# Row sums of two Strassen-type FFNs made pair by pair, a first up unit in 8 products, and squares added on VectorE

## The reference, cut to what matters

```python
def _swiglu(h, w1, w3, w2):
    return (jax.nn.silu(h @ w1) * (h @ w3)) @ w2          # FFN2: D_FF = 2816

u = rmsnorm(x, norm_mlp_g[i]) @ w_up[i]                   # FFN3: D_FF_2 = 4096
x = x + jnp.square(jax.nn.relu(u)) @ w_down[i]
```

```python
xf * lax.rsqrt(jnp.mean(xf * xf, axis=-1, keepdims=True) + EPS)
```

## Time and profile before

| What | Value |
|---|---|
| Median of 3 runs | 3257.37 us (3256.01 to 3264.33) |
| The profiled execution, its own time | 3262.65 us |
| Its span in the trace | 3261.0 us |
| TensorE matmuls busy | 3027.8 us (93%) |
| DVE, ACT, POOL busy | 1029.3, 445.8, 416.3 us |
| FFN2, first to last unit start | 1550.84 to 1967.56 us |
| FFN3, first to last unit start | 2734.95 to 3145.63 us |

### The profile page before, as it was taken

One profiled execution on the slowest core, in us unless ns is written; L12 is line 12 of the kernel. 1 busy time (PEld: TensorE's weight loads), 2 busy tenths in 40 slices (PEclk: granted clock), 3 DMA queues, 4 the chain that ended last, 5 costly groups with the idle time before them and its releaser, 6 DMA issues.

```text
span 3261.0 us, 26581 instructions
## 1 busy us (share of the span) xinstructions
PE 3027.8 (93%) x10626; PEld 1897.7 (58%) x10626; DVE 1029.3 (32%) x1857; ACT 445.8 (14%) x968; POOL 416.3 (13%) x362
## 2 busy tenths in 40 slices
PE   3999999997999999998999998997889998999998
PEld 1555555553556457443888884754444445888873
DVE  6222225004005534002332335107550003343432
ACT  2000000002004334002100001004330000000001
POOL 0000000000002000001344440000000002444420
PEclk8999999998999999999999999998999999999999
DMA  6222224111110100221222221210002221222211
GB/s 249 88 98 99 101 99 135 66 55 39 52 45 8 30 20 11 78 78 51 78 79 89 78 78 57 72 67 14 26 28 83 77 78 65 78 78 78 78 58 58
DMA packets 42521, 228.10 MB, mean 70 GB/s; under 512 B 4144, under 2 KB 6448, under 8 KB 26928
## 3 DMA queue, kind: packets, MB, share of 16 engines
q1 hardware_dynamic: 32768, 181.17, 16.6%
q0 software_dynamic: 8928, 39.85, 3.4%
q10 hardware_dynamic: 720, 5.61, 0.4%
HBM read 224.51 MB, written 2.10 MB: 69 GB/s over the span
## 4 chain that ended last, share of the span: by engine, by line
PE 88%; DVE 8%; ACT 1%; issue 1%; DMA 1%; ACTq 0%; DVEq 0%
PE banks L365 57%; PE banks L430 21%; PE banks L537 1%; PE banks L692 1%; PE banks L612 1%; PE banks L685 1%; DMA consts_sb<-consts 1%; PE banks L374 1%; DVE rstd L1259 1%; PE banks L835 1%; DVE scratch_b L1276 1%; PE banks L602 1%; DVE p_embed L1309 1%; PE banks L417 1%; DVE big L1355 1%
## 5 line engine op out<-in xcount | busy, mean ns | idle before, releaser
L365 PE MATMUL banks<-normed,weight_ring 128*128 128x512 f32 (+2 forms) x3296 | 1199.8, 523 | 49.3 <-ACT normed L916 29.9
L365 PEld LDWEIGHTS banks<-normed,weight_ring 128*128 128x128 f32 (+1 forms) x3296 | 630.6, 192 | 601.5 <-issue 551.7
L365 PE MATMUL banks<-big,weight_ring 128*128 128x512 f32 (+4 forms) x1720 | 626.5, 519 | 8.5 <-DVE big L1448 5.6
L365 PEld LDWEIGHTS banks<-big,weight_ring 128*128 128x128 f32 (+2 forms) x1720 | 321.0, 187 | 300.7 <-issue 273.6
L430 PE MATMUL banks<-big 128*128 128x256 f32 x1776 | 414.4, 389 | 39.1 <-DVE rpb_rows L1370 32.3
L430 PEld LDWEIGHTS banks<-big 128*128 128x128 f32 x1776 | 345.9, 195 | 92.0 <-DVE rpb_rows L1370 25.1
L1825 POOL TENSOR_TENSOR big<-weight_ring 128x512 f32<-128x512 f32 (+1 forms) x66 | 82.7, 1253 | 1216.1 <-PE banks L430 542.4
L430 PE MATMUL banks<-big,weight_ring 128*128 128x256 f32 x736 | 170.9, 381 | 0.0
L430 PEld LDWEIGHTS banks<-big,weight_ring 128*128 128x128 f32 x736 | 140.9, 191 | 19.5
L1309 DVE CUSTOM_DVE_ANT_0 p_embed<-big,rpb_rows 128x1024 f32<-128x1024 f32 x116 | 141.9, 1223 | 24.6 <-DMA big<-w_ada 16.5
L1445 DVE TENSOR_TENSOR scratch_a<-scratch_a,banks 128x512 f32<-128x512 f32 x16 | 11.0, 688 | 356.9 <-ACT scratch_a L1001 356.9
(11 more groups left out here) (261 smaller groups left out, 2435.8 us busy)
## 6 DMA issues: line engine op xcount, KB each, us to landing
weight_ring<-weights SPq DMA_DIRECT2D x136, 1024.0 KB, 4.9
big<-w_ada POOLq DMA_DIRECT2D x42, 512.0 KB, 4.1
weight_ring<-weights SPq DMA_DIRECT2D x20, 768.0 KB, 4.2
weight_ring<-weights SPq DMA_DIRECT2D x16, 704.0 KB, 4.1
big<-w_ada POOLq DMA_DIRECT2D x4, 2048.0 KB, 26.0
rpb_rows<-w_ada POOLq DMA_DIRECT2D x14, 512.0 KB, 4.7
weight_ring<-weights SPq DMA_DIRECT2D x8, 640.0 KB, 3.9
residual<-xT ACTq DMA_DIRECT2D x2, 1536.0 KB, 20.1
```

The lines of the kernel that those rows point to most:

```text
L365: ins = nc.tensor.matmul(o, w, r, start=start, stop=stop)
```

## The change

1. **Pairing.** The two halves of the inner tiles are no longer the first and the last `kp` tiles but the even and the odd ones. A pair of neighbouring tiles can then give its four sums (128x256 each) as soon as both tiles exist. POOL reads the weights with a stride of two tiles; the loads are unchanged.
2. **Pair sums.** DVE makes the four chained operations of a pair (`pair_sums`) right behind the up unit that completes it: after every second up unit in FFN2 (f odd), after every up unit in FFN3. Sums of `HR[0]` and `HR[1]` have a buffer each (one of the four sums is written in place over rows that are no longer needed, another partly in free ends of scratch tensors). The `row_sums` calls between the phases go away.
3. **First unit.** The first up unit of each FFN is made without sums: 16 matmuls of 512 columns, k outermost, two PSUM banks, each k waiting only for its tile of H. The row sums of H (`all_sums`, six operations) are made during it. ACT and DVE finish it with full-width operations (`first_up2`, `first_up3`).
4. **Squares.** In `down1` and `out1` DVE copies the first squared chunk and adds the next six in `TMP`; TensorE makes one ones-matmul per column part from that total and one from the last chunk. `out2` keeps its sums on TensorE.
5. Some semaphores are shared between norms to make room (three `stages` of "norm_late", with bases).

The diff, cut to its core:

```diff
@@ tensor
-                    if sums and not (peel and j == 0):
+                    if sums and sums[0] is not g and not (peel and j == 0):
...
-            def fast(v, rows, t, rows_sem=None, rows_at=0, t_at=None):
+            def fast(v, rows, buffer, totals=None, freed=None):
...
+                def raw(m, j):
+                    return lambda p: slot(n, (m * 2 * kp + 2 * p + j) * P, P)
...
+                def rows_raw(j, l):
+                    return lambda p: rows[:, 2 * p + j, l * HALF:(l + 1) * HALF]
...
+                if freed is not None:
+                    pe.wait_ge(hid, freed)
+                product(za, raw(0, 0), rows_raw(0, 0), True, True)
                 pe.wait_ge(sums, v + 1)
-                if t_at is not None:
-                    pe.wait_ge(hts, t_at + 2)
-                product(zb, w[1], total(1), True)
-                product(zc, w[0], total(0), True)
-                if t_at is not None:
-                    pe.wait_ge(hts, t_at + 3)
+                if totals is not None:
+                    pe.wait_ge(hts, totals)
+                product(zb, total(1), rows_total(1), True)
+                product(zc, total(0), rows_total(0), True)
                 pe.wait_ge(took, 5 * v + 1)
-                product(zb, w[2], total(2), False)
+                product(zb, total(2), rows_total(2), False)
...
+            def first_up(n, s, g):
+                begin(n)
+                for k in range(KC):
+                    pe.wait_ge(g["ready"], g["base"] + k + 1)
+                    for w in range(2):
+                        last = mm(bank[:, 3 * s + w, :], slot(n, (w * KC + k) * P, P), H[:, k, 0:S], k == 0,
+                                  k == KC - 1, k == 0 and w == 0)
+                last.then_inc(first_done, 1)
...
+                if sg is g:
+                    pe.wait_ge(sg["sq_used"], sg["base"] + KC - 1)
+                    for (a, b, _), q in zip(parts, banks):
+                        nc.tensor.matmul(bank[:, q, 0:b - a], ones, TMP[:, 0, a:b], start=True, stop=False)
+                    pe.wait_ge(sg["sq"], sg["base"] + KC)
+                    for (a, b, _), q in zip(parts, banks):
+                        last = nc.tensor.matmul(bank[:, q, 0:b - a], ones, SQ[:, 1, a:b], start=False, stop=True)
...
-            fast_up(range(34, 38), nmlp, 16)
-            fast_up(range(38, 42))
-            fast_down(42, 0, HT, 26, 20)
...
+            first_up(UP3[0], (V_UP3[1] + 1) % 2, nmlp)
+            fast_up([V_UP3[j] for j in range(1, 8)], FF + 1, TOTALS_3[0])
+            fast_down(V_DOWN3[0], 0, FF + 4, TOTALS_3[1])
...
@@ scalar
+            def first_up2(s):
+                act.wait_ge(first_done, 1)
+                A(bias_t[:, 5 * s * HALF:(5 * s + 2) * HALF], bank[:, 3 * s, :], ACT.Silu).then_inc(first_act, 1)
+            def first_up3(s):
+                act.wait_ge(first_done, 2)
+                for w in range(2):
+                    A(HR[0][:, w, :], bank[:, 3 * s + w, :], ACT.Relu).then_inc(first_act, 1)
...
@@ vector
+                def each(i, a, b):
+                    for p, n in groups(i):
+                        V.tensor_tensor(row_sum(buffer, rows, i, p, n), a(p, n), b(p, n),
+                                        ALU.subtract).then_inc(hts, 1)
+                        row_sums_done[0] += 1
+                    return row_sums_done[0]
...
+                at = each(2, lambda p, n: raw(1, 1, p, n), lambda p, n: raw(0, 1, p, n))
+                if buffer < 2:
+                    dve.wait_ge(hts, at)
+                at = each(0, lambda p, n: raw(0, 1, p, n), lambda p, n: raw(0, 0, p, n))
+                dve.wait_ge(hts, at)
+                at = each(1, lambda p, n: raw(1, 1, p, n), total(0))
+                dve.wait_ge(hts, at)
+                each(3, lambda p, n: raw(1, 0, p, n), total(1))
+
+            def pair_sums(i, p):
+                dve.wait_ge(dve_c, chain[0])
+                row_sums_of(i % 2, HR[i % 2], lambda i: [(p, 1)])
+
+            def all_sums():
+                row_sums_of(2, H, lambda i: [(0, 4)] if i > 1 else [(0, 2), (2, 2)])
...
@@ up2_unit
+                if f % 2 == 1:
+                    dve.wait_ge(hid, f + 1)
+                    pair_sums(f // PHASE, f % PHASE // 2)
@@ up3_unit
                 V.scalar_tensor_tensor(rows, rows, 0.0, rows, ALU.max, ALU.mult).then_inc(hid, 1)
+                dve.wait_ge(hid, FF + j + 1)
+                pair_sums(j // 4, j % 4)
...
+            def squares_added(g, width):
+                at = g["base"]
+                dve.wait_ge(g["sq"], at + 1)
+                V.tensor_copy(TMP[:, 0, 0:width], SQ[:, 0, 0:width]).then_inc(g["sq_used"], 1)
+                for o in range(1, KC - 1):
+                    dve.wait_ge(g["sq"], at + o + 1)
+                    dve.wait_ge(g["sq_used"], at + o)
+                    V.tensor_tensor(TMP[:, 0, 0:width], TMP[:, 0, 0:width], SQ[:, o % 2, 0:width],
+                                    ALU.add).then_inc(g["sq_used"], 1)
```

More of the change, by code:

```diff
@@ L80, with _fast, _ups, _downs @@
 DOWN3 = [SEQ["down3a"], SEQ["down3b"], SEQ["down3c"], SEQ["down3d"]]
[L84 to L92, removed]
-def unit_of(v):
[L96 to L103, removed]
+FAST = []
+def _fast(n, kp, copied):
+    FAST.append((n, kp, copied))
+    return len(FAST) - 1
+def _ups(units, a, b):
+    return {f: _fast(units[f], 4, True) for f in range(a, b)}
+def _downs(units, i, kp, copied):
+    return [_fast(units[i] + m, kp, copied) for m in range(4)]
+V_UP2 = _ups(UP2, 1, 16)
+V_DOWN2 = [_downs(DOWN2, 0, 4, True)]
+V_UP2.update(_ups(UP2, 16, FF))
+V_DOWN2 += [_downs(DOWN2, 1, 4, False), _downs(DOWN2, 2, 3, False)]
+V_FFN3 = len(FAST)
+V_UP3 = _ups(UP3, 1, 8)
+V_DOWN3 = [_downs(DOWN3, 0, 4, False)]
+V_UP3.update(_ups(UP3, 8, 12))
+V_DOWN3.append(_downs(DOWN3, 1, 4, False))
+V_UP3.update(_ups(UP3, 12, 16))
+V_DOWN3 += [_downs(DOWN3, 2, 4, False), _downs(DOWN3, 3, 4, False)]
+V_END = len(FAST)
+TOTALS_2 = [6 + 4 * n for n in (0, 4, 8, 11)]
+TOTALS_3 = [TOTALS_2[-1] + 6 + 4 * n for n in (0, 4, 8, 12, 16)]
+def unit_of(v):
+    return FAST[v][0:2]
 def copied_upto(v):
-    return sum(1 for u in range(v + 1) if not any(at <= u < at + 4 for at in V_DOWN2[1:] + V_DOWN3))
+    return sum(1 for u in range(v + 1) if FAST[u][2])
 def _places(columns):
@@ L464, in fast @@
                 pe.wait_ge(took, 5 * v + 3)
-                product(zc, w[3], raw(1, 1), False)
-            def fast_up(vs, normed=None, t_at=None):
-                for v in vs:
[L469 to L477, removed]
+                product(zc, total(3), rows_raw(1, 1), False)
@@ new lines, in first_up, with fast_up @@
+            def first_up(n, s, g):
[6 more added lines that the diff above has]
+                last.then_inc(first_done, 1)
+            def fast_up(vs, hidden=None, totals=None):
+                for i, v in enumerate(vs):
+                    fast(v, H, 2, totals if i == 0 else None, hidden if i == 1 else None)
@@ L479, in squares_total, with fast_down @@
+            def fast_down(vs, i, hidden, totals):
+                pe.wait_ge(hid, hidden)
+                for v in vs:
+                    fast(v, HR[i % 2], i % 2, totals)
             def squares_total(g):
@@ L706, in _ @@
             norm_sums(nb, LAT)
[L708 to L713, removed]
+            first_up(UP2[0], (V_UP2[1] + 1) % 2, nb)
+            fast_up([V_UP2[f] for f in range(1, 16)], 1, TOTALS_2[0])
+            fast_down(V_DOWN2[0], 0, 8, TOTALS_2[1])
+            fast_up([V_UP2[f] for f in range(16, FF)])
+            fast_down(V_DOWN2[1], 1, 16, TOTALS_2[2])
+            fast_down(V_DOWN2[2], 2, 22, TOTALS_2[3])
             squares_total(sq2)
@@ L964, in up2_units @@
                     u2, g1 = tmps(v % 2)[1], tmps(v % 2)[4]
+                    if v == V_UP2[1] + 1:
+                        act.wait_ge(hid, 1)
                     fast_snap(v)
@@ L1500, in _ @@
             link(gate_coef(GATE3, 8, 0.5, 5))
+            squares_added(down1, T)
             dve.wait_ge(down1["free"], KC)
@@ L1594, in _ @@
             merge(mrg1, MR1)
+            squares_added(out1, S)
             dve.wait_ge(out1["free"], 2 * KC)
```

223 lines of the change are left out of this document (110 added, 113 removed).

## The result

The changed kernel takes **3270.28 us** (median of 7 runs, 3269.56 to 3273.73) against 3257.68 for the kernel before (7 runs, 3256.01 to 3264.33): ratio 1.0036, interval 1.0024 to 1.0047, so 12.6 us slower, just past the 9.8 us that a measurement can tell. The profiled spans are 3268.3 us and 3261.0. They differ by 7.3 only, since the profiled execution of before stood 5.0 above the median; sums made from the two traces go against the 7.3.

The account below looks back on a forecast made before the run. TensorE was taken as the bound; 67.2 us removed, 66.6 us of stalls and 8.6 us of clock falls added gave +8.0 us on the 3257.37 median: 3265 us, range 3218 to 3287, most of the chance within 3252 to 3273.

Parts of the forecast that it names:

- The junctions' 47.4 us: Seven FFN units where TensorE waited for row sums: their extra time goes, 47.4 us less.
- the squares' 12.9: Unhidden ones-matmuls in down1 and out1 fall to one on the DVE total: 12.9 us less.
- B1: Rival: pair operations cost a flat 0.755 us, gaps of about 1 us, no clock falls; 3219 us, chance 0.12.
- B2: Rival: pair operations are hidden, at 0.425 us each; 3192 us, chance 0.08.
- D: Rival: openings or squares bring nothing, or a down unit still waits for its totals; 3285 us, chance 0.05.
- POOL's L1828 and L1830 lines longer by about 0.2 us: Sign of being right: these two POOL weight-sum lines lengthen by about 0.2 us.
- Openings: First units of both FFNs: 16.4 us each against 19.74 and 19.89, 6.9 us gained for both.
- Stalls: Fourth product late behind pair sums: 2.9 us 15 times in FFN3, 2.1 us 11 times in FFN2; 66.6 us added.
- the clock: FFN3 stalls let TensorE's clock fall in 6 of 15, at 1.43 us each: 8.6 us added.
- FFN2's part: Clock cost of FFN2's gaps of 1.7 us before the fourth product: put at nothing.
- case A: Forecast case: DVE and POOL take turns, some clock falls; 3257 us without falls, 3271 with ten; chance 0.55.
- C: Rival: the clock falls in nearly every FFN3 stall, 1.43 to 2.64 us each; 3287 us, chance 0.20.

Follow-up runs that it names:

- experiment 6: The kernel before with only the squares of down1 and out1 added on DVE: 3250.10 us, ratio 0.9969.
- Experiments 1 and 2: Changed kernel with POOL starting weight sums three products later: 3191.84 us; changed kernel with pair sums moved behind the next unit's emptying of zb: 3195.52 us.
- experiment 3: Changed kernel with five unread matmuls before the wait of the fourth product in 15 FFN3 units: 3251.84 us, ratio 0.9974.
- experiment 7: The kernel before with POOL starting a unit's weight sums after product 3 of the previous unit: 3221.49 us, ratio 0.9886.

## Why the prediction was right, and where it was off

**Right in the mechanism.** The junctions' 47.4 us went as worked out, and so did the squares' 12.9 (experiment 6 alone: 12.6). The four operations took turns with POOL: 1.37 three times and 0.42, as predicted, starting at U + 2.69 for U + 2.66. The rivals B1 and B2 are excluded by those durations and by the stalls, D by the openings and by experiment 6. Experiments 1 and 2 show the cause: the durations hang on POOL, the time on L1453's place behind them. One point failed: "POOL's L1828 and L1830 lines longer by about 0.2 us". L1924 took 1.44 us in that unit and L1926 1.32, where POOL's operations take 1.27 undisturbed: 0.17 and 0.05 longer, so 0.2 only for the two together.

**Sizes by step.** Openings: 8.0 us gained for 6.9. Against the 13.74 us at full speed, FFN3's (16.33) lost 2.6 and FFN2's (15.33) 1.6, after 5.14 and 5.80 us of idleness; the 2.64 for a slow start, taken from the PLE opening, was right in FFN3 and too much in FFN2. Stalls: 2.65 and 1.87 us for 2.9 and 2.1, so 60.4 for 66.6. Part of that is L1453, which starts 0.08 before the drawn end of the last pair operation (2767.28 against 2762.72 + 4.64 = 2767.36), where I had it 0.04 after; it ends at U + 7.67 for the 7.82 worked out.

**The mis-sized term is the clock.** "Two in five of 15 is 6, at 1.43 each 8.6 us" became 11 at 1.68, 18.5 us, as the trace shows and experiment 3 gives back. The chance of a fall was taken from five single gaps in stages of different work, and two falls in five say little of a rate. The 1.43 was one row's. FFN2's part, "I put at nothing", came out right: none of 11. But one of its reasons was misread, "of the eight like them (1.85 to 1.87) most left the clock up". Six of those gaps stand before L537 in the trace of before, and within 1.6 us of TensorE's return the granted clock was down after five of them, left up only by the one at 2284.06. The windows view from one of the five and from that one:

```profile
2236.82:2244.00 7.18, 6.72 (x46) 4.09 (x46) 6.13 (x23) 3.65 (x15) 0.00 (x0) 0.76 0.01 2
```

```profile
2284.00:2291.00 7.00, 5.57 (x46) 3.21 (x46) 6.48 (x27) 4.09 (x18) 0.00 (x0) 1.00 0.01 2
```

The stage of these gaps has more and shorter bursts of matmuls than FFN2. Read rightly, its rows spoke for falls in FFN2, and that none came there was luck.

By these steps the sum is -47.4 - 8.0 - 12.9 + 39.8 + 20.6 + 18.5 = +10.6 us for the +8.0 predicted; with -3.1 in stages whose code did not change it is 7.5, beside the 7.3 of the spans. That the total came so near is in part luck: stalls that were 6.2 us cheaper and openings that were 1.1 us better than predicted hid most of the 9.9 us that the clock cost more. So it is case A as to the time ("with ten 3271"), with the falls in number on C's side of its point ("from eight falls on"), at a price near the lower end of C's. Compared by the medians of 7 runs the kernel is 12.6 us slower, past the 0.3%, and the forecast of "same" was on the wrong side of that line by 2.8 us; the clock's 9.9 us were enough to carry it there. Against the medians beside the experiments (7.6 to 8.6 us) it was on the right side.

**What stays open.** Why 4 of 15 equal stalls of 2.38 us left the clock up was not tried. No run moved a gap on purpose, but two did so in passing. The gap of 2.82 us in the earlier trace rows (1464.95) left the clock up, 14.00 us for its 32 records. In experiment 7, whose code is the same up to there, it came 2.8 us sooner and the clock fell (first row below). The gap of 3.69 us in FFN2 was followed by a fall in the kernel before (second row, granted clock 0.66 in the 5 us from there), and by none in experiment 6 (third row, 1.00):

```profile
1462.12 15.45 PE L365 MATMUL banks<-big,weight_ring 128*128 128x512 f32 x32 [2.82 <-DVE big L1448]
```

```profile
1895.44 2.38 PE L430 MATMUL banks<-big 128*128 128x256 f32 x8 [3.69 <-DVE rpb_rows L1370]
```

```profile
1885.09 1.97 PE L430 MATMUL banks<-big 128*128 128x256 f32 x8 [3.69 <-DVE rpb_rows L1379]
```

So the same gap behind the same work goes either way. That leaves the moment at which it comes as the likely cause, which is argued and not shown. The Trainium skill, TensorE: Matmul & The Clock Gate, "What's actually happening", says that TensorE's activity is looked at in a window that runs on by itself, whatever the kernel does. The mixed outcomes of equal gaps agree with that. It ties the fall to an idle stretch longer than the gaps of 1.95 and 2.38 us that let the clock fall here; there the measurement decides. The openings were not run alone; their gain is read from the trace.

## What to carry to other kernels

Before short VectorE operations are put beside another engine's work, look at whether that engine is GpSimd reading SBUF and the VectorE operations have two inputs in SBUF, as all that were stretched here (those that empty PSUM kept their 0.42 us): then count each one as itself plus the whole GpSimd operation it meets, and look for what is queued behind them. The cure costs one number or one moved call: start GpSimd's share after VectorE's deadline, or make the VectorE share after the operation that TensorE waits for. And a stall of TensorE that cannot be removed can be made cheaper by matmuls that nobody reads, if they leave a gap that lets the clock stay up: 1.52 us was short enough here, 1.95 was not.

## What was not expected of the hardware

- **A sharp step in the idle time.** Inside the dense matmuls of the two FFNs, gaps of 1.52 us and of 1.59 to 1.78 us let the clock fall in none of 26, gaps of 1.95 in 10 of 15, gaps of 2.38 in 11 of 15. A fall costs 1.68 us in a unit of 12.09. Shortening the gap from 2.38 to 1.95 gave nothing, from 1.95 to 1.52 all 18 us. It is no limit for other stages: where the matmuls were less dense, five of six gaps of 1.86 to 1.87 us had a fall behind them (trace of before, 2236 to 2298).
- **Who is first by 0.03 or 0.04 us decides who waits** when DVE and POOL meet (experiment 7), and with it 1.25 us of TensorE's time.
- **One number in POOL's wait** was worth 40 us in the kernel before and 78 in the changed one; the 78 are more than all that the change was made to remove (47.4 + 8.0 + 12.9 = 68.3 us).
